# Inverting 64x64 triangular blocks on half of the columns per level

## The reference

```python
def step(state, inp):
    r_t, w_t, k_t, v_t, kk_t, a_t = inp
    sa = jnp.einsum('bhvk,bhk->bhv', state, -kk_t)
    state = (state * w_t[:, :, None, :]
             + sa[..., None] * (kk_t * a_t)[:, :, None, :]
             + v_t[..., None] * k_t[:, :, None, :])
    return state, jnp.einsum('bhvk,bhk->bhv', state, r_t)
...
_, y = lax.scan(step, s0, seq_major)
```

## Time and profile before

| | us |
|---|---|
| median of 3 runs | 1694.86 |
| lowest and highest of them | 1693.37, 1698.76 |
| the profiled execution | 1689.58 |
| its span on the core | 1687.8 |
| levels of round 1, in that span | 240.9 to 266.8 |
| the four rounds | 182 to 420 |

### The profile page before, as it was taken

The page is one execution under the profiler, slowest core; times in us unless marked ns, Lnnn a source line. Parts: engine busy times, 40 slices in busy tenths (PEclk is TensorE's granted clock), DMA queues, the critical chain, the costliest instruction groups (busy, mean ns, idle before and its releaser), DMA issues.

```text
span 1687.8 us, 26133 instructions
## 1 busy us (share of the span) xinstructions
PE 1525.4 (90%) x10702; PEld 1272.3 (75%) x10702; DVE 1093.8 (65%) x1661; ACT 705.6 (42%) x1057; POOL 58.9 (3%) x52
## 2 busy tenths in 40 slices
PE   5999888988989999999989989999999888778892
PEld 4889666866768888888868778787799666777882
DVE  5831766676479737737679997454765446567775
ACT  5422434433444333333444222334344346357773
POOL 0000000000000000000000000000000000222221
PEclk9999889998989999999989999999999999689996
DMA  6220000002412222222312222232243203569896
GB/s 245 100 100 1 2 2 3 3 2 75 151 53 97 101 100 100 100 89 90 122 50 100 100 75 100 77 135 88 88 150 128 72 26 122 192 222 364 322 329 219
DMA packets 37828, 189.69 MB, mean 112 GB/s; under 512 B 4304, under 2 KB 4432, under 8 KB 24400
## 3 DMA queue, kind: packets, MB, share of 16 engines
q1 hardware_dynamic: 30672, 167.08, 28.2%
q0 software_dynamic: 4864, 16.78, 2.7%
q10 hardware_dynamic: 2176, 4.19, 0.7%
HBM read 175.46 MB, written 12.58 MB: 111 GB/s over the span
## 4 chain that ended last, share of the span: by engine, by line
PE 70%; DVE 17%; DMA 6%; ACT 4%; issue 3%; POOL 0%; DVEq 0%; SPq 0%; POOLq 0%; ACTq 0%
PE acc L470 18%; PE acc L472 18%; PE acc L471 18%; DMA raw<-wstream 4%; DVE CA L2382 3%; PE acc L712 2%; DVE wl L1915 2%; PE mb L712 1%; PE mb L614 1%; DVE wl L1903 1%; PE mb L545 1%; PE acc L1015 1%; ACT wh L1230 1%; PE mb L470 1%; PE mb L472 1%
## 5 line engine op out<-in xcount | busy, mean ns | idle before, releaser
L470 PE MATMUL acc<-XH,wh 128*128 128x512 f32 x1008 | 397.3, 394 | 5.9 <-DVE wl L1915 4.9
L472 PE MATMUL acc<-XH,wl 128*128 128x512 f32 x1008 | 393.1, 390 | 0.0
L471 PE MATMUL acc<-XL,wh 128*128 128x512 f32 x1008 | 392.8, 390 | 0.0
L1230 ACT ACTIVATE wh<-raw 128x2048 fp32r<-128x2048 f32 x99 | 189.4, 1915 | 248.2 <-DMA raw<-wstream 248.2
L1915 DVE TENSOR_TENSOR wl<-raw,wh 128x2048 fp32r<-128x2048 f32 x99 | 226.0, 2287 | 71.7 <-ACT wh L1230 68.5
L470 PEld LDWEIGHTS acc<-XH,wh 128*128 128x128 f32 x1008 | 189.7, 188 | 48.1 <-DVE wl L1915 5.8
L471 PEld LDWEIGHTS acc<-XL,wh 128*128 128x128 f32 x1008 | 189.7, 188 | 41.1 <-issue 2.2
L472 PEld LDWEIGHTS acc<-XH,wl 128*128 128x128 f32 x1008 | 189.5, 188 | 39.9
L1251 ACT ACTIVATE ev<-acc 128x512 f32<-128x512 f32 x146 | 85.7, 598 | 217.8 <-PE acc L472 197.1
L1903 DVE TENSOR_TENSOR wl<-raw,wh 128x1024 fp32r<-128x1024 f32 x96 | 117.0, 1223 | 47.2 <-ACT wh L1217 40.9
L1217 ACT ACTIVATE wh<-raw 128x1024 fp32r<-128x1024 f32 x96 | 101.4, 1060 | 35.9 <-DMA raw<-wstream 35.3
(11 more groups left out here) (524 smaller groups left out, 2739.9 us busy)
## 6 DMA issues: line engine op xcount, KB each, us to landing
raw<-wstream SPq DMA_DIRECT2D x99, 1024.0 KB
raw<-wstream SPq DMA_DIRECT2D x96, 512.0 KB
YG<-YT ACTq DMA_DIRECT2D x8, 512.0 KB
XT<-xT SPq DMA_DIRECT2D x2, 1024.0 KB, 9.6
XT<-xT SPq DMA_DIRECT2D x1, 2048.0 KB, 7.8
XD<-HN SPq DMA_DIRECT2D x4, 512.0 KB, 2.6
out<-XTK SPq DMA_DIRECT2D x4, 512.0 KB, 2.6
cst<-consts SPq DMA_DIRECT2D x1, 1230.0 KB, 18.3
```

The lines of the kernel that those rows point to most:

```text
L470: mm(out_, a[0], b[0], start=start, stop=False)
L471: mm(out_, a[0], b[1], start=False, stop=False)
L472: return mm(out_, a[1], b[0], start=False, stop=stop)
L1230: actv(wh[:, n % RING].rearrange("p a b c -> p (a b c)"), raw[:, n % RING, :], ACT.Copy).then_inc(hi_done, 1)
```

## The change

All five levels take 32 of 64 columns. Two views name them: `blocks(a, l)` cuts the columns of `a` in pieces of 2^l, and `block_cols(a, l, odd)` takes the even or the odd ones of these pieces. For level 1 the pieces are 2 columns wide with gaps of 2, for level 5 one piece of 32.

```diff
+            def by_quarters(out_, left, right, l, a):
+
+                for t in range(TT):
+                    for c in range(2):
+                        o = out_[hp(c), t * HALF:(t + 1) * HALF]
+                        last = mm(blocks(o, l), left(hp(c), t), block_cols(right(hp(c), t), l, a), start=True, stop=True)
+                return last
+
...
                         pe.wait_ge(s["rk_tm"], 6 * ct * 2 + 2 * (l - 1) + hh + 1)
-                        by_halves(bank(hh, 0), lambda p, t: NR[p, hh, t, 0, :],
-                                  lambda p, t: Tm[p, hh, t, :]).then_inc(s["rk_q"], 1)
-                        turn_t(hh)
+                        by_quarters(bank(hh, 0), lambda p, t: NR[p, hh, t, 0, :],
+                                    lambda p, t: Tm[p, hh, t, :], l, 0).then_inc(s["rk_q"], 1)
+                        turn_t(hh, l - 1)
...
-                        by_halves(bank(hh, 0), lambda p, t: TTm[p, hh, t, :],
-                                  lambda p, t: Qm[p, hh, t, :]).then_inc(s["rk_t"], 1)
+                        for t in range(TT):
+                            for c in range(2):
+                                last = mm(bank(hh, 0)[hp(c), t * HALF:(t + 1) * HALF], TTm[hp(c), hh, t, :],
+                                          Qm[hp(c), hh, t, 0:HALF], start=True, stop=True)
+                        last.then_inc(s["rk_t"], 1)
...
-                        actv(flat(TTm[:, hh]), turn_bank(hh), ACT.Copy).then_inc(s["rk_tte"], 1)
+                        if l == 1:
+                            last = actv(flat(TTm[:, hh]), turn_bank(hh), ACT.Copy)
+                        else:
+                            last = actv(block_cols(flat(TTm[:, hh]), l - 1, 1),
+                                        blocks(turn_bank(hh)[:, 0:TT * HALF], l - 1), ACT.Copy)
+                        last.then_inc(s["rk_tte"], 1)
...
-                        v.tensor_tensor(Qm[:, hh], by_tok(bank(hh, 0)[:, 0:TT * HD]), lv(l),
+                        v.tensor_tensor(Qm[:, hh, :, 0:HALF], by_tok(bank(hh, 0)[:, 0:TT * HALF]), lv(l),
                                         ALU.mult).then_inc(s["rk_qm"], 1)
...
-                        v.tensor_tensor(Tm[:, hh], Tm[:, hh], by_tok(bank(hh, 0)[:, 0:TT * HD]),
-                                        ALU.add).then_inc(s["rk_tm"], 1)
+                        T = block_cols(Tm[:, hh].rearrange("p a b -> p (a b)"), l, 0)
+                        v.tensor_tensor(T, T, blocks(bank(hh, 0)[:, 0:TT * HALF], l), ALU.add).then_inc(s["rk_tm"], 1)
```

More of the change, by code:

```diff
@@ L20 @@
 LEVELS = 6
+HALF = HD // 2
 D_FF = 2816
@@ L73 @@
          ("w_router", KT * 20), ("b_router", 20), ("lam", 4 * HD)]
-CCOLS = [("ident", P), ("ones", P), ("blk", P), ("eps", 8), ("alibi", S), ("mask_nr", 2 * HD), ("mask_lv", LEVELS * HD),
-         ("reset", S), ("spare", S), ("id64", HD), ("invcnt", 4 * POOL_PAD), ("rank", 4),
+CCOLS = [("ident", P), ("ones", P), ("blk", P), ("eps", 8), ("alibi", S), ("mask_nr", 2 * HD), ("mask_lv", HD + (LEVELS - 1) * HD // 2),
+         ("reset", S), ("spare", S + (LEVELS - 1) * HALF), ("id64", HD), ("invcnt", 4 * POOL_PAD), ("rank", 4),
          ("upto", P), ("count", P), ("token", 2 * TT), ("base", 16)]
@@ L87, with blocks, block_cols @@
         "s7": ["sums", "more"], "y": ["root"], "mu": ["ends"]}
+def blocks(a, l):
+    return a.rearrange("p (n b) -> p n b", b=2 ** l)
+def block_cols(a, l, odd):
+    return a.rearrange("p (n a b) -> p n a b", a=2, b=2 ** l)[:, :, odd, :]
 def offsets(cols):
@@ L714, in by_halves, with turn_t @@
                 return last
-            def turn_t(hh):
-                by_halves(turn_bank(hh), lambda p, t: Tm[p, hh, t, :],
-                          lambda p, t: ident[p, p]).then_inc(s["rk_tt"], 1)
+            def by_quarters(out_, left, right, l, a):
[4 more added lines that the diff above has]
+                return last
+            def turn_t(hh, l):
+                if l == 0:
+                    last = by_halves(turn_bank(hh), lambda p, t: Tm[p, hh, t, :], lambda p, t: ident[p, p])
+                else:
+                    last = by_quarters(turn_bank(hh), lambda p, t: Tm[p, hh, t, :], lambda p, t: ident[p, p], l, 1)
+                last.then_inc(s["rk_tt"], 1)
             def level(l):
@@ L758, in run @@
                             pe.wait_ge(s["rk_tm"], 12 * ct + 10 + hh + 1)
-                            turn_t(hh)
+                            turn_t(hh, LEVELS - 1)
                 return run
@@ L2125, in lv @@
             def lv(l):
-                return cs("mask_lv", l * HD, (l + 1) * HD).unsqueeze(1).to_broadcast([P, TT, HD])
+                if l == 0:
+                    return cs("mask_lv", 0, HD).unsqueeze(1).to_broadcast([P, TT, HD])
+                o = HD + (l - 1) * HALF
+                return cs("mask_lv", o, o + HALF).unsqueeze(1).to_broadcast([P, TT, HALF])
             def nr(ct):
@@ L2911, in constants @@
     lv = [((ih >> l) % 2 == 1) & ((jh >> l) % 2 == 0) & (ih >> (l + 1) == jh >> (l + 1)) for l in range(LEVELS)]
+    lv = lv[:1] + [m[:, (np.arange(HD) >> l) % 2 == 0] for l, m in enumerate(lv) if l]
     cnt = [np.minimum(np.arange(POOL_PAD) + 1, 2 ** (g + 1)) for g in range(4)]
@@ L2915, in constants @@
         "ident": i == j, "ones": np.ones((P, P)), "blk": same, "alibi": np.where(c <= i, c - i, -1e30),
-        "mask_nr": np.concatenate([ih < jh, ih <= jh], axis=1), "spare": np.zeros((P, S)),
+        "mask_nr": np.concatenate([ih < jh, ih <= jh], axis=1), "spare": np.zeros((P, S + (LEVELS - 1) * HALF)),
         "mask_lv": np.concatenate(lv, axis=1), "reset": np.broadcast_to(np.arange(S)[None] % HD != 0, (P, S)),
```

## The result

The changed kernel takes 1710.96 us (median; 1708.54 to 1717.36), the kernel before 1694.11 us in the same comparison (1693.36 to 1698.76). The ratio is 1.010, with a 95% interval of 1.0066 to 1.0133. So the change makes the kernel slower by some 17 us, beyond the upper end of the range (1701). The profiled execution took 1717.36 us, 27.8 us more than that of before. That is more than the 17 us between the medians because the trace of after is its slowest execution and the trace of before (1689.58 us) lies under its median.

The account below looks back on a forecast made before the run. TensorE was taken as the bound, its narrowed batches paced by weight loads. Gains of 1.5 + 0.9 + 0.4 = 2.8 us less 1.5 us for one low clock stretch gave -1.3 us: 1693.6 us, range 1686 to 1701.

Parts of the forecast that it names:

- one more low stretch, +1.5 us: Behind round 2's pair sums the clock falls as in round 1, one low stretch more, costing 1.5 us.
- the second rival: In levels 1 to 5 the clock falls for lack of streamed columns; six low stretches give 1701 us; chance 12%.
- the 2.8 us: Gain before the clock's cost: 1.5 from copies, 0.9 after level 5, 0.4 from DVE in round 0.
- The rival's ceiling, ten stretches: The clock is low for a third of the levels' time, ten stretches: +12.6 us, 1707 us.
- Pace unchanged at 29 ns a record, loads as the limit: In TensorE's narrowed batches weight loads set the pace, so 29 ns a record stays; at best 1.3 us won.
- Columns set the pace after all: Rival: halved columns halve TensorE's narrowed batches, 0.23 us saved on each, 1673 us; chance 7%.
- Fine pieces at no cost: Pieces of 2 columns at level 1 cost nothing; the rival, slow pieces, gave 1701 us, chance 4%.
- Copies: ACT's `TTm` copies fall from 384 to 275 ns; with earlier batch ends, 0.135 us won 11 times, 1.5 us.
- Round 0: Gains in round 0: copies at levels 2 and 5, level 3's late `Qm` 0.4 us, 0.22 us after level 5.
- the end: After level 5 the chain runs over ACT; two shorter `TTm` copies before the exponentials win 0.22 us a round.
- DVE busy time falls by 10 us without effect: Shorter DVE products and additions save 10.7 us of DVE time, nearly none of it on the path.
- A low stretch behind the pair sums of round 2: Sign that the forecast is right: round 2 loses its clock behind the pair sums as round 1 does.

Follow-up runs that it names:

- after_pairs: Changed kernel, all three products still narrow, with only level 1's pair sums streaming 64 columns instead of 2: 1695.08 us.
- q_twice_12: Changed kernel with each product Q streaming its 32 columns twice in levels 1 and 2 alone: 1693.31 us.
- w_all: Changed kernel with TensorE taking all 64 columns again in Q, transpositions and T' x Qm; masks, copies and additions stay at 32: 1695.77 us.
- pairs_twice_12: Changed kernel with pair sums at 64 columns and Q's 32 columns streamed twice in levels 1 and 2: 1694.42 us.

## Why the prediction was wrong

The step that failed is "one more low stretch, +1.5 us". The mechanism was named, with its price and its direction, and the sign of the second rival (12%), a clock of 0.50 in levels 2 to 5, came true. Its mechanism did so only in part: the levels don't lose the clock of themselves (round 0, `after_pairs`), they fail to bring it back. What was mis-sized is the count: within the rounds the profiled execution had 113 us at the low clock and not 44, some twenty short stretches more instead of one. At the predicted 1.54 us each, less the 2.8 us, they make 28 us, and the profiled execution lost 27.8. That it fits so closely is partly luck: 1.54 us for a stretch of 3.4 is 0.45 for each us, the levels lost 0.40, and 10 us more at the low clock lie behind the rounds.

The error behind the count is a picture: each place was taken to need its own columns, so that a fall at the pair sums ended with them and only "around the pair sums" was at risk. The trace of before held a hint: its one fall behind level 1 ended one stretch later, at 249.3, and by then the wide side work and 0.8 us of level 2 had run (this line of its chain is where level 2 begins):

```profile
248.47 1.48 PE acc L712 x32
```

It was not asked what ends a fall. `after_pairs` and `q_twice_12` show the answer: narrow levels keep a clock that they have, but where it fell just ahead of them they didn't bring it back for 20 and 34 us in rounds 2 and 1. The rival's ceiling, ten stretches, came from the same picture.

Point by point:

- *Pace unchanged at 29 ns a record, loads as the limit*: right at the high clock (188.22 to 188.69). At the low one 16 records take 0.85 us, 53 ns each, with the same 32 columns. "Columns set the pace after all" (7%) is out.
- *Fine pieces at no cost*: right. The transposing batch of level 2, pieces of 2 columns, takes 0.47 us as every other.
- *Copies*: 279 ns (275 predicted) in the profile of after. Ahead of `mb<-Qm,TTm` the idle time was to fall from 3.0 to near 1.5 us; it is 1.9 us in `w_all` and 1.8 us in `after_pairs`, where the clock is up, so some 1.2 us are won and not 1.5. In after it is 1.3 us, which is no gain of the copies but the slower TensorE.
- *Round 0*: two copies (0.27), level 3's `Qm` (0.4) and the end (0.22) make 0.89 us, and the chain gave 0.89 us. The parts fit less well: level 2's copy and `Qm` gave 0.51 us (0.535 forecast), level 5's copy 0.16 (0.135), the end 0.13 (0.22), since one of its copies now waits for TensorE's last transposition, and 0.09 came in between from no term of the sum. So the exact match is luck, and the sum of 2.8 us is right in size only; in the time it couldn't be seen, since the versions that keep the clock measure within 0.3% of before, either way.
- *DVE busy time falls by 10 us without effect*: 1084.7 us instead of 1093.8, 9.1 us less.
- *A low stretch behind the pair sums of round 2*: there is one, 20.5 us long.
- *The range*: it was built for up to six stretches. The rule of the Trainium skill cited in the second rival ("TensorE: Matmul & The Clock Gate", section "What's actually happening"), a clock throttled by default and released by activity, names this direction: the low level is where TensorE stays until something lifts it. The trace agrees only if activity means something else than busy time, since 34.10 of 34.10 us busy didn't lift it. The forecast used only half of that rule, what makes the clock fall.

What stays open: why Q alone at 64 columns gives everything back (1693.66 us) and the transpositions or T' x Qm alone, with as many columns each, half or less (1701.92 and 1705.16 us). The traces say only where the difference lies, in the low stretches behind level 1 (6.8 us against 20.5 and 20.4). Nor was it tested why `pairs_twice_12` had its clock down for longer in the carrying phase. That small shifts in time decide such places is only argued, from the spread of 16 us among its executions.

## What to carry to other kernels

Where TensorE's pace is set by weight loads, as here (0.47 us a batch with 64 columns or with 32), moving columns are free in time, and taking them away can cost: look at the granted clock before cutting columns that nobody waits for. Then look not only at where the clock falls but at what stands behind that place and would have to bring it back; thin work right behind a fall was the expensive kind here. A free filler at the place of the fall (wider sums, 1.83 against 1.81 us) or right behind it restored the time, but only to that of the kernel before.

## What the runs showed of the hardware

- TensorE can be busy for 34.10 of 34.10 us with a granted clock of 0.50 throughout. Busy time doesn't bring the clock back, and columns that are streamed for nothing do: 1711 us became 1696 with them.
- The same narrow levels ran at 1.00 for 20 us and more (round 0 of after, rounds 1 and 2 of `after_pairs`) and at 0.50 for 34 us (round 1 of after). In `after_pairs` nothing but the pair sums differs from after.
- At the low clock the weight loads slow down too: a batch of 16 small records takes 0.85 us instead of 0.47.
